# Expert weights and sums one pair of slots behind the dots, one activation function table for a half step of attention, and operands loaded a stage ahead

## The reference

```
h = rmsnorm(x);  q, k, v, gates = split(h @ w_in)
A: stick-breaking attention, 8 heads x 64:
   z = q.k / 8;  log_keep = -softplus(z) where k_pos < q_pos, else 0
   weight = exp(log_sigmoid(z) + sum of log_keep over later keys before the query)
B: sliding window attention, 8 q heads / 2 kv heads x 64, distance bias, a sink
M: cross attention, 4 heads x 128, to 256 memory tokens
x += (sum over branches sigmoid(gate) * (o @ w_o)) @ w_out
experts: q = rmsnorm(x) @ w_q;  8 heads pick 16 of 128*128 experts each by two top-16 lists
   a = gelu(u_tab[idx] . x);  x += sum over 128 slots of softmax weight * a * v_tab[idx]
```

## Time and profile before

| | |
|---|---|
| median of 3 runs | 4818.94 us (4816.24 to 4823.6) |
| the profiled execution | 4819.45 us |
| its span, first to last instruction | 4817.7 us |
| PE busy | 3634.3 us, 75% |
| DVE busy | 2936.3 us, 61% |
| POOL busy | 2011.2 us, 42% |
| ACT busy | 1702.6 us, 35% |
| HBM traffic | 1448.48 MB by DMA, mean 301 GB/s |

### The profile page before, as it was taken

The page is one execution under the profiler, slowest core; times in us unless marked ns, Lnnn a source line. Parts: engine busy times, 40 slices in busy tenths (PEclk is TensorE's granted clock), DMA queues, the critical chain, the costliest instruction groups (busy, mean ns, idle before and its releaser), DMA issues.

```text
span 4817.7 us, 34691 instructions
## 1 busy us (share of the span) xinstructions
PE 3634.3 (75%) x10561; PEld 1921.8 (40%) x10561; DVE 2936.3 (61%) x6134; ACT 1702.6 (35%) x3098; POOL 2011.2 (42%) x1542
## 2 busy tenths in 40 slices
PE   7996689876665588888467766688887577777777
PEld 4544455532332344454233434444454233233222
DVE  1130321396764688769866655679669877577554
ACT  2111510237774423333488733323332211111111
POOL 0000000164444366766645434466766633333332
PEclk9997799987787789999788776699999799989999
DMA  4323023587766599999977666699999899999998
GB/s 163 106 68 111 30 79 108 216 349 295 258 253 246 189 366 415 421 422 395 372 266 274 247 245 261 257 379 395 420 420 370 332 422 421 421 419 416 422 422 356
DMA packets 269916, 1448.48 MB, mean 301 GB/s; under 512 B 28432, under 2 KB 70160, under 8 KB 116112
## 3 DMA queue, kind: packets, MB, share of 16 engines
q0 software_dynamic: 165888, 1208.03, 62.6%
q1 hardware_dynamic: 103840, 238.22, 13.6%
HBM read 1400.93 MB, written 46.14 MB: 300 GB/s over the span
## 4 chain that ended last, share of the span: by engine, by line
POOL 32%; issue 25%; DMA 13%; PE 12%; DVE 5%; ACT 2%; SPq 0%; POOLq 0%; ACTq 0%; DVEq 0%
POOL side L1013 18%; POOL ring L1002 14%; DMA ring<-in_experts_dram,idx 12%; PE ps L1284 4%; PE ps L1211 3%; DVE ring L1676 2%; PE ps L1217 1%; PE ps L1232 1%; PE ps L1136 1%; PE ps L1255 1%; DMA work<-mem_scratch 1%; PE ps L1170 1%; ACT diag L1423 1%; ACT work L1345 0%; PE ps L1154 0%
## 5 line engine op out<-in xcount | busy, mean ns | idle before, releaser
L1002 POOL DMA_INDIRECT ring<-in_experts_dram,idx x1152 | 1105.8, 960 | 2769.0 <-PE ps L1284 1684.0
L1284 PE MATMUL ps<-ring,diag 128*128 128x512 f32 x3072 | 1637.4, 674 | 702.7 <-ACT diag L1423 674.2
L1676 DVE CUSTOM_DVE_ANT_0 ring<-ring,ps 128x1024 f32<-128x1024 f32 x1152 | 1373.3, 1217 | 371.7 <-DMA ring<-in_experts_dram,idx 354.6
L1284 PEld LDWEIGHTS ps<-ring,diag 128*128 128x128 f32 x3072 | 617.3, 212 | 1535.4 <-ACT diag L1423 894.4
L1013 POOL TENSOR_TENSOR side<-side,ring 128x1024 f32<-128x1024 f32 x384 | 904.8, 2356 | 8.1
L1415 ACT ACTIVATE act_<-hid 128x2 f32<-128x2 f32 x576 | 117.2, 204 | 1772.7 <-DVE hid L1676 1771.5
L1681 DVE TENSOR_TENSOR wgt<-act_,gw 128x2 f32<-128x2 f32 x576 | 322.7, 560 | 491.1 <-ACT act_ L1415 491.1
L1428 ACT ACTIVATE ring<-ring,wgt 128x1024 f32<-128x1024 f32 x384 | 434.9, 1133 | 0.0
L1211 PE MATMUL ps<-work 128*128 128x384 f32 x1152 | 399.7, 496 | 41.2 <-DMA work<-hT_scratch 41.2
L1423 ACT ACTIVATE diag<-const,wgt 128x128 f32<-128x128 f32 x768 | 287.6, 398 | 361.9 <-DVE wgt L1681 360.6
L1211 PEld LDWEIGHTS ps<-work 128*128 128x128 f32 x1152 | 224.3, 195 | 218.6 <-issue 47.4
(11 more groups left out here) (177 smaller groups left out, 3540.6 us busy)
## 6 DMA issues: line engine op xcount, KB each, us to landing
work<-in_w_gate_o_dram SPq DMA_DIRECT2D x72, 768.0 KB, 8.3
work<-in_w_q_dram SPq DMA_DIRECT2D x24, 1024.0 KB, 8.5
ring<-in_experts_dram,idx POOLq DMA_INDIRECT x1152, 12.2
work<-in_w_out_dram SPq DMA_DIRECT2D x12, 1024.0 KB, 9.1
w_qkv<-in_w_in_dram SPq DMA_DIRECT2D x5, 2048.0 KB, 9.6
work<-k_scratch SPq DMA_DIRECT2D x37, 256.0 KB, 4.7
work<-v_scratch SPq DMA_DIRECT2D x37, 256.0 KB, 4.3
o_x<-q_scratch SPq DMA_DIRECT2D x9, 768.0 KB, 8.8
```

Of the source, the lines that this page charges most:

```text
L1002: i = nc.gpsimd.indirect_dma_start(out=ring[:, j % RING, :], out_offset=None, in_=A["experts"], in_offset=bass.IndirectOffsetOnAxis(ap=idx ...
L1284: last = nc.tensor.matmul(acc[:, h, :], diag[:, (by_pe(j) - 1) % 4, :], ring[:, j % RING, DM + h * HB:DM + (h + 1) * HB], start=(j % SLOTS ...
L1676: last = nc.vector.tensor_tensor_reduce(out=u, in0=u, in1=xp, scale=1.0, scalar=0.0, op0=ALU.mult, op1=ALU.add, accum_out=hid[:, j % SLOTS ...
```

## The change

1. **One pair behind.** In pair Q, VectorE makes the dots of pair Q and then the product of pair Q-1 (`product`). ScalarE takes the gelu of Q, then makes the diagonals and scaled rows of Q-1 (`spread`), then runs the front's steps. TensorE runs the front's steps of Q, then accumulates Q-1. The end of a tile (`finish`) moves from pair 0 to pair 1 of the next tile, and one last round follows pair 575.
2. **One table.** Before Abs, Exp and Ln of a half step ScalarE loads the function set that holds Exp and Ln together.
3. **Loads ahead.** `work` is cut anew, so that the operands of the windows (bias, `mkT`, `mv`, `kswT`, `vsw`) stand beside those of attention A, and `hx` with one half of `wbuf` beside those of the windows. For groups 0 and 1, SP starts the window loads at step 0 and `hx` with the first weight block at `win_at`; for group 2, which also has the caches, they stay at `win_at` and `gate_at`.
4. **Steps and costs.** Attention A of groups 1 and 2 starts at step 5 and not 1; for group 2 five steps lie before the first window and five before the first gate unit, for the others one each. The costs that deal the steps out rise: 5.2 for 4.5 in attention A, 2.4 for 2.0 in the windows, and 2.0 for steps that only wait for loads.

```diff
-        b = 1
+        b = self.stick_at = 5 if g else 1
+        self.sampled = self.base + self.n == NT
...
-        b = self.win_at + 2
+        b = self.wins_at = self.win_at + (5 if self.sampled else 1)
...
-        self.gate_at = g0 = max(self.wkeep) + 1
+        self.gate_at = max(self.wkeep) + 1
+        g0 = self.gate_at + (3 if self.sampled else -1)
...
-            c += 4.5 * (tau in self.zscore or tau in self.suffix)
-            c += 2.0 * (self.win_at + 2 <= tau < self.gate_at)
+            c += 2.0 * (tau < self.stick_at or self.win_at <= tau < self.wins_at or self.gate_at <= tau < g0 + 2)
+            c += 5.2 * (tau in self.zscore or tau in self.suffix)
+            c += 2.4 * (self.wins_at <= tau < self.gate_at)
...
                         for k in range(min(3, f.nkeys)):
                             load_v(f, k)
-                        if f.base + n == NT:
+                        if not f.sampled:
+                            load_win(f)
+                        if f.sampled:
                             sp.dma_start(kcache, A["cache_kT"]).then_inc(kc_in, 16)
...
                     if tau == f.win_at:
                         sp.wait_ge(st_kept, f.tiles0 + n)
...
+                        if f.sampled:
+                            load_win(f)
+                        else:
+                            load(f, 0)
+                            for i in range(n):
+                                sp.dma_start(hx[:, i], hT_d[f.base + i]).then_inc(h_in, 16)
...
             advance(0)
-            for m in range(NT):
-                for q in range(NB):
-                    advance(1 + m * NB + q)
-                    accumulate(m, q)
+            for Q in range(NT * NB + 1):
+                if Q < NT * NB:
+                    advance(1 + Q)
+                if Q:
+                    accumulate((Q - 1) // NB, (Q - 1) % NB)
...
                         a = za[:, x % 2]
+                        nc.scalar.preload_act_table_set("natural_log_exp_and_others")
                         nc.scalar.activation(a, ps[:, 4 + x % 3, :], ACT.Abs).then_inc(absd, 1)
...
+            for Q in range(NT * NB + 1):
+                m, q = Q // NB, Q % NB
+                if Q < NT * NB:
                     c = slice(q * BATCH, (q + 1) * BATCH)
-                    act.wait_ge(dots, m * NB + q + 1)
+                    act.wait_ge(dots, Q + 1)
                     nc.scalar.activation(act_[:, c], hid[:, c], ACT.Gelu_apprx_tanh).then_inc(gelus, 1)
...
+                if Q:
+                    spread((Q - 1) // NB, (Q - 1) % NB)
+                if Q < NT * NB:
+                    advance(1 + Q)
...
                     last.then_inc(dots, 1)
-                    dve.wait_ge(gelus, m * NB + q + 1)
-                    c = slice(q * BATCH, (q + 1) * BATCH)
-                    nc.vector.tensor_tensor(wgt[:, c], act_[:, c], gw[:, m % 2, c], ALU.mult).then_inc(weights, 1)
+                    if m or q:
+                        product(m * NB + q - 1)
```

More of the change, by code:

```diff
@@ L847, in load_v, with load_win @@
                 sp.dma_start(vbuf[:, at % 3], v_d[f.steps_[k][2]]).then_inc(v_in[at % 3], 16)
+            def load_win(f):
+                g, n = f.g, f.n
+                sp.dma_start(bias.rearrange("p h k -> p (h k)"), wide_dram[:, 0:BW]).then_inc(bias_in, 16)
+                first = 0 if g else 1
+                for src, dst in ((0, kswT), (1, vsw)):
+                    v = sw_d[f.base - 1 + first:f.base + n, :, src].rearrange("t p c -> p t c")
+                    sp.dma_start(dst[:, first:n + 1], v).then_inc(win_in, 16)
+                sp.dma_start(mkT.rearrange("p h m -> p (h m)"), mem_d[:, 0]).then_inc(win_in, 16)
+                sp.dma_start(mv.rearrange("p k m -> p (k m)"), mem_d[:, 1]).then_inc(win_in, 16)
             def load_vm(b):
@@ L922, in front @@
                         sp.wait_ge(w_kept, f.win1)
-                        for i in range(2):
-                            load(f, i)
-                        for i in range(n):
-                            sp.dma_start(hx[:, i], hT_d[f.base + i]).then_inc(h_in, 16)
+                        if f.sampled:
+                            load(f, 0)
+                            for i in range(n):
+                                sp.dma_start(hx[:, i], hT_d[f.base + i]).then_inc(h_in, 16)
+                        load(f, 1)
                     if tau in f.unit:
@@ L1410, in _, with spread @@
             advance(0)
-            for m in range(NT):
-                for q in range(NB):
+            def spread(m, q):
+                act.wait_ge(weights, m * NB + q + 1)
+                for j in range(m * SLOTS + q * BATCH, m * SLOTS + (q + 1) * BATCH):
+                    if sided(j):
+                        continue
+                    d = by_pe(j) - 1
+                    if d >= 4:
+                        act.wait_ge(pe_done, d - 3)
+                    last = nc.scalar.activation(diag[:, d % 4, :], ident, ACT.Copy, scale=wgt[:, j % SLOTS:j % SLOTS + 1])
+                last.then_inc(diags, 1)
+                for j in range(m * SLOTS + q * BATCH, m * SLOTS + (q + 1) * BATCH):
+                    if sided(j):
+                        v = ring[:, j % RING, DM:2 * DM]
+                        nc.scalar.activation(v, v, ACT.Copy, scale=wgt[:, j % SLOTS:j % SLOTS + 1]).then_inc(scaled, 1)
@@ L1413, in _ @@
+            for Q in range(NT * NB + 1):
+                m, q = Q // NB, Q % NB
+                if Q < NT * NB:
                     c = slice(q * BATCH, (q + 1) * BATCH)
-                    act.wait_ge(dots, m * NB + q + 1)
+                    act.wait_ge(dots, Q + 1)
                     nc.scalar.activation(act_[:, c], hid[:, c], ACT.Gelu_apprx_tanh).then_inc(gelus, 1)
-                    act.wait_ge(weights, m * NB + q + 1)
-                    for j in range(m * SLOTS + q * BATCH, m * SLOTS + (q + 1) * BATCH):
-                        if sided(j):
-                            continue
-                        d = by_pe(j) - 1
-                        if d >= 4:
-                            act.wait_ge(pe_done, d - 3)
-                        last = nc.scalar.activation(diag[:, d % 4, :], ident, ACT.Copy, scale=wgt[:, j % SLOTS:j % SLOTS + 1])
@@ L1424, in _ @@
-                    last.then_inc(diags, 1)
-                    for j in range(m * SLOTS + q * BATCH, m * SLOTS + (q + 1) * BATCH):
-                        if sided(j):
-                            v = ring[:, j % RING, DM:2 * DM]
-                            nc.scalar.activation(v, v, ACT.Copy, scale=wgt[:, j % SLOTS:j % SLOTS + 1]).then_inc(scaled, 1)
-                    advance(1 + m * NB + q)
+                if Q:
+                    spread((Q - 1) // NB, (Q - 1) % NB)
+                if Q < NT * NB:
+                    advance(1 + Q)
@@ L1653, in front, with product @@
                     yield
+            def product(Q):
+                m, q = Q // NB, Q % NB
+                dve.wait_ge(gelus, Q + 1)
+                c = slice(q * BATCH, (q + 1) * BATCH)
+                nc.vector.tensor_tensor(wgt[:, c], act_[:, c], gw[:, m % 2, c], ALU.mult).then_inc(weights, 1)
             def finish(m):
@@ L1667, in _ @@
                 dve.wait_ge(x_in, 16 * (m + 1))
+                if m:
+                    dve.wait_ge(dots, m * NB)
                 nc.vector.tensor_copy(xp, xrow[:, :]).then_inc(x_taken, 1)
@@ L1691, in _ @@
                         weigh(m + 1, None)
-                    if q == 0 and m:
+                    if q == 1 and m:
                         finish(m - 1)
                     advance(1 + m * NB + q)
+            product(NT * NB - 1)
             finish(ST)
```

21 lines of the change are left out of this document (7 added, 14 removed).

## The result

The changed kernel takes 4569.15 us (median of 4 runs, 4555.76 to 4583.34), the kernel before 4821.27 us in the same session (4816.24 to 4825.49): a ratio of 0.9478, 95% interval 0.9445 to 0.9511. The forecast was 4500 us with a range of 4400 to 4640. Sign and range held, but 4569 lies outside the forecast case's own 4450 to 4560, and it is nearer to the rival's 4600 than to 4500; of the gain of 319.5 us that was forecast, 252 came. The profiled execution of after took 4562.79 us, 256.7 less than that of before, and with that one the terms are compared.

The account below looks back on a forecast made before the run. Gathers were taken as DMA-bound at about 420 GB/s, with ScalarE fullest in attention A's valley; 170 + 36.5 + 50 + 24 + 5 + 39 - 5 = 319.5 us off 4819.45 gave 4500 us, range 4400 to 4640.

Parts of the forecast that it names:

- the forecast case: Whole kernel: the prediction's main case, 4500 us with its own range of 4450 to 4560, given a chance of 0.52.
- the rival's 4600: TensorE takes ACT's place: clock stays 0.79, half-step pairs take 9.2 us, windows give back less; 4600 us, chance 0.22.
- Attention A, 170 us forecast: Attention A, groups 1 and 2: shorter stretches save 56.5 and 83.5 us, added pairs 20 and 10; together 170 us.
- the 8.0 us for a pair with a half step: Attention A: ACT's new floor of 6.9 us plus the old 1.1 on top; bounds 7.0 and 9.2.
- 6.9 by ACT, 4.5 by GpSimd: Attention A: floor with a half step, 9.46 less two table loads; without one, GpSimd's 4.3 us plus small gaps.
- The excess of 1.1: Attention A: half-step pairs 1.1 to 1.2 us above ACT's 9.46, put down to uneven top lists and TensorE's turn.
- The clock and TensorE: Attention A: diagonal waits become short, so the granted clock rises from 0.79 towards 0.94 and TensorE's 7.35 us becomes 6.2.
- ACT under 75%: Attention A of group 1: signs expected in the changed profile, ACT busy below 75% and PE above 80%.
- The coupling goes too: Rival: the 1.1 excess in attention A vanishes, and about half the remaining window waits; 4410 us, chance 0.17.
- Windows, 36.5 and 50 forecast: Windows, groups 1 and 2: operand waits go, half the gelu waits go, added pairs cost less; 36.5 and 50 us.
- Gate loads, the start, the rest: Gate loads save 24 us; two load waits and 13 table loads before the loop 39; gelu waits from 943 to 1113, 5.
- The ring, 5 us forecast: Ring: each slot stays one pair longer, leaving DMA idle now and then in the gates; costs 5 us, between -10 and 40.

Follow-up runs that it names:

- Experiment 11: The changed kernel with the top list's third piece cut over two pairs, except in attention A of group 1, the control: 4539.96 us.
- experiment 2: The changed kernel without the load of the common function table ahead of the half step: 4648.09 us.
- experiment 1: The changed kernel without the one-pair lag; product, diagonals and sums back in the round of their own dots: 4668.03 us.
- experiment 3: The changed kernel with window operands and `hx` loaded where they were before, the empty steps kept: 4619.6 us.
- Experiments 8 and 9: Both: the changed kernel with the product on ScalarE instead of VectorE. The first keeps the lag, 4534.07 us; the second has no lag, 4487.57 us.
- experiment 8: The changed kernel, lag kept, with the product made by ScalarE as two Copies instead of by VectorE: 4534.07 us.

## Why the forecast was right, and where it was off

**Attention A, 170 us forecast.** By the forecast's own reckoning, with 5.0 us for each added pair, group 1 gained 373 + 20 - 334 = 59 us (76.5 forecast) and group 2 441 + 10 - 372 = 79 (93.5): 138 us. So the term came out 32 us short. Its mis-sized part is the 8.0 us for a pair with a half step. By the same formula it is (334 - 17 x 4.5) / 30 = 8.6 us and (372 - 19 x 4.5) / 34 = 8.4. Measured one by one, from dots to dots, the reason shows (a half step is counted to the pair in whose list its scores stand; its last steps can fall into the next pair, so that pairs without one are not free of it):

```
mean us (pairs)      half step    half step and third top piece   none
before, group 1      8.19 (20)    12.27 (7)                       6.24 (9)
after,  group 1      6.73 (21)    12.81 (6)                       4.32 (11)
before, group 2      8.12 (28)    16.01 (4)                       6.18 (11)
after,  group 2      6.42 (27)    15.15 (5)                       3.90 (12)
```

The table runs from the first half step to the last, without those two pairs, and leaves out pairs with a third top piece and no half step: 17.91 us (1 pair), 13.84 (2), 16.42 (2) and 12.09 (2).

The change took 1.5 to 1.7 us from pairs with a half step and 1.9 to 2.3 from pairs without, and these ended at or below what I had expected (6.9 by ACT, 4.5 by GpSimd). So the split of the old time was wrong at both ends: pairs without a half step took 6.2 us and not 4.5, and those with one, lumps apart, 8.1 to 8.2 and not 10.5 to 10.7. The change took next to nothing from the pairs with a half step and a third top piece (12.27 to 12.81 us and 16.01 to 15.15); the few with such a piece and no half step are shorter. The excess of 1.1 was no even tax, as I had it: a good part of it sits in these lumps, and they have hardly moved. One in the timeline of after, all engines (start, us, instruction; the bracket is the idle time before it and its releaser):

```profile
1170.54 1.98 PE L1299 MATMUL ps<-ring,diag 128*128 128x512 f32 x4
...
1172.14 2.35 POOL L1028 TENSOR_TENSOR side<-side,ring 128x1024 f32<-128x1024 f32 x1
...
1172.51 2.03 DVE L1485 TENSOR_SCALAR part<-flat 128x16 uint32<-128x16 uint32 x1
...
1177.19 2.47 DVE L1494 SCALAR_TENSOR_TENSOR idx<-e 128x16 uint32<-128x16 f32 x1
1177.27 2.35 POOL L1028 TENSOR_TENSOR side<-side,ring 128x1024 f32<-128x1024 f32 x1
1179.69 1.22 DVE L1707 CUSTOM_DVE_ANT_0 ring<-ring,ps 128x1024 f32<-128x1024 f32 x1
...
1182.10 0.20 ACT L1448 ACTIVATE act_<-hid 128x2 f32<-128x2 f32 x1 [6.40 <-DVE hid L1707]
...
1182.64 3.78 PE L1299 MATMUL ps<-ring,diag 128*128 128x512 f32 x4 [8.02 <-ACT diag L1436]
```

VectorE goes from the dots that end at 1169.30 to the next at 1179.69 with nothing but one product (0.47 us) and the top list. Two operations of the list, L1485 and L1494, take 2.03 and 2.47 us here and 0.17 where no add of GpSimd meets them. ScalarE waits 6.40 us for those dots and TensorE 8.02 for a diagonal that belongs to the pair before them: product and diagonal stand behind the new dots in both lists, so a lagged pair is only as loose as the next dots are punctual. Experiment 11 takes the lumps apart in group 2; its pairs with a lump fall by 5 us, the program gains 29 and the control does not move, which shows the lumps as a cause of part of the excess.

The forecast of 170 us was also right in part by luck. It built attention A's gain from the table loads alone, two of 1.28 us for each of 64 half steps, 164 us, and gave the lag no term of its own there. By the stage table the loads are worth 24 + 45 = 69 us in attention A (experiment 2) and the lag 28 + 48 = 76 (experiment 1). The sum of 145 is near the 138 that came, since what was too much for the loads stood in for what was missing for the lag.

**The clock and TensorE.** I expected TensorE's clock to go from 0.79 to about 0.94 and its waits for the diagonal to become short. The clock came to 0.85 and 0.84, and in after TensorE still waits 75.3 us for diagonals from 1091 to 1425 (78.0 before), in 24 pieces of up to 10.8 us against 20 of up to 11.3. So the step from the order of the lists to short waits and a high clock failed: the waits stayed, and the clock rose by 0.06 and 0.04 and not by 0.15. The forecast of ACT under 75% held, PE above 80% did not (71% in group 1, 80% in group 2). The rival of 4600, with TensorE in ACT's place, fits in the total and not in its mechanism: by the forecast's own formula a half step's pair takes 8.4 to 8.6 us, not 9.2, and its clock of 0.79 did not stay. (In the rival *The coupling goes too*, half of the waits that remain in the windows is (88.6 - 45) / 2 = 22 us and not 26, so its sum is 4414.) Neither sign of a wrong mechanism came: the last stretch runs at 413 GB/s and not below 410, and the half-step pair is not above 9.3 us.

**Windows, 36.5 and 50 forecast.** Group 1: 183 + 10 - 159 = 34 us, right. Group 2: 262 + 20 - 263 = 19; by the stage table, with five more pairs, it is 286 + 25 - 285 = 26, and the scatter of that stage makes either uncertain by some 15. The 17.8 us of waiting for operands did not go; in group 2 the loads have not moved, and the three empty steps more, which I had counted as time enough, went by without sparing it (19.0 us).

**Gate loads, the start, the rest.** The wait for `hx` went in every group (41.2 us to 0.8), and experiment 3 prices all the moved loads at 50 us. The forecast's sum for them, without group 2, was 20.5 + 14 + 22.5 = 57; by stages they came to 16 before the loop, 22 in the windows and 13 in the gates of group 1. Before the loop 39 us were forecast and 31 came (943 to 912); of these 11 hang on the table and 16 on the loads, by experiments 2 and 3.

**The ring, 5 us forecast.** This is the worst term. Experiments 8 and 9 differ by the lag alone and put it at 47 us, above even the upper bound of 40. Where the DMA is the bound it costs little, 5 us in the last 200 pairs, as the landing margin of the earlier trace rows had it. By stages 10 + 13 us lie in the two gate stretches, where the prediction looked for them, and 6 + 10 in attention A. These are the uneven stretches, in which one pair of reserve fewer can be felt; that the lumps are what makes them so is argued and not shown. With the 99 us net of experiment 1, the lag's relief of VectorE would be about 146 us; this sum takes the two effects as additive, which is argued and not measured.

**What is left open.** Why experiment 8 gave attention A of group 2 nothing, although it took load off VectorE there. What the added empty steps are worth. And whether a lag with product and diagonal *ahead* of the next dots, which would free them from a lump, keeps the relief without the hold; it was not tried.

## What to carry to other kernels

Moving a dependent step one round back takes its wait away but holds the buffers of that round; where buffers are few, look first whether the step can go to the engine that produces its input, which took both wait and hold away here (4488 us against 4569). Count the reserve of a ring in its most uneven stretch too, and not only in its smooth one: two places fewer cost 28, 72 and 231 us in three kernels whose last 200 pairs, with 10 places, take 1018 to 1026 us in all three. And split a mean time per round into its kinds before a floor is put under it: here pairs with a half step took 8.2 us, those with a lump as well 12 to 16, and the change hardly touched the second kind. And price each part of a change by itself, also where one part seems to explain the whole.

## What the runs showed of the hardware

A VectorE operation with two inputs in SBUF stands while GpSimd adds. The product of 128x2 takes 0.15 us alone; in the timeline of after one that meets an add ends with it:

```profile
1145.95 2.87 DVE L1682 TENSOR_TENSOR wgt<-act_,gw 128x2 f32<-128x2 f32 x1
1146.44 2.35 POOL L1028 TENSOR_TENSOR side<-side,ring 128x1024 f32<-128x1024 f32 x1
```

Of the 576 products 187 took over 0.3 us, and all of them overlap an add and end with it, within 0.03 us (before: 176 of 176). The one shown began 0.49 us before its add and did not get through either. That holds for 32 of the 187, which began up to 0.63 us ahead of the add, while GpSimd issued a gather; the five that began 0.66 to 0.80 us ahead took 0.15 us. The dots, with one input in SBUF and one in PSUM, were not touched: 183 began within an add and none was longer than 1.22 us. The lump above shows that an operation with one uint32 input in SBUF (L1485, 2.03 us) can stand the same way. The product alone has 370 us of busy time for 576 x 0.15 = 86 us of work. So a short operation on VectorE that meets a GpSimd add can cost more than the add's whole 2.36 us, 3.01 at the most here, and VectorE's 90% in attention A are in part such standing: the products of those 48 pairs of group 1 hold VectorE 42 us longer than 0.16 us each would.

The Trainium skill agrees on the cause: "GPSIMD Engine Reference", section "1. Specifications", row "SBUF interfaces", has GpSimd share them with VectorE, with contention for VectorE instructions in a 2-port perf mode or with two SBUF inputs. This trace agrees for the product, which has two, and shows what such a meeting costs, 2.87 us in the row above.

As for the function table, the activation behind a load again starts about 0.02 us after its end, and experiment 2 shows no second price. The Trainium skill's 1380 ns of drain ("ScalarE: Activation LUTs", "What ACT_TABLE_LOAD costs") is not borne out in any run here.
